# Rows of blocks 2 to 5: added through diagonals and fp32 products, or two of sixteen by VectorE, in place of accumulated transposes

## The chip, the core and the metric

The kernel runs on one core of a Trainium2 chip. The metric is the device time of one execution in microseconds; lower is better. The profile is one execution recorded by the hardware profiler.

## The reference

The reference is a trunk of two layers over 512 tokens of 1024 channels, all in fp32. Layer 0 mixes the tokens by gated spatial products and sparse attention, layer 1 by a gated linear recurrence (HGRN2) of eight heads. After each mixer comes PEER: every token scores 2 x 128 keys in 8 heads, keeps the 16 best experts of 16384 per head, and adds their outputs:

```
experts = top 16 of (s_top[0][i] + s_top[1][j])      # per token and head
gate    = softmax(best)
act     = gelu(sum_d x[t, d] * u_tab[experts, d])    # one number per token and expert
x      += sum over 128 experts of gate * act * v_tab[experts]
```

So each token gathers 128 rows of u and 128 rows of v (1024 floats each) in each layer. A last RMS norm ends the trunk.

## The kernel before

Tokens lie on the 128 partitions. The work is cut into 1024 slots: slot s is one expert of each of 128 tokens. 128 slots make a block (`BLOCK`; 128 tokens of one layer, blocks 0 to 3 for layer 0, 4 to 7 for layer 1), 16 slots a routing unit, and 256 slots a phase (`PHASE`). In every slot:

- POOL (L677) issues an indirect DMA that gathers, for 128 tokens, the u and v rows side by side (8 KB each, 1 MB in all) into one of 8 buffers of `region_g`. Before it issues slot s, it waits until slot s - 8 has been freed (`row_freed`).
- DVE (L1323) multiplies the u half with the normed tokens and sums: the dot product.
- ACT (L943, L944) takes its gelu and multiplies it with the gate, which gives the weight of the row.
- Then the weighted v half is added to the block's sum, in one of three ways. By diagonal: ACT (L956) writes an identity scaled by the weight into `diag`, and PE (L1845) multiplies it with the v half in two fp32 products of 512 columns that accumulate in two PSUM banks. By VectorE (`on_dve`): DVE (L1332) adds weight times v to `x_res`, two slots later, and frees the buffer. By transposes (blocks in `TURNED`, 2 to 5): ACT (L951) scales the 1024 values of the v half in place, and PE (L1851) takes it through eight accumulating 128 x 128 transposes.

Before the change, slots 0 to 191 have VectorE add rows 5, 7, 9 and 13 of each sixteen (`ATTENDED_ROWS`), all other rows of blocks 0, 1, 6 and 7 go by diagonal, and blocks 2 to 5 go by transposes alone. The sum of such a block lies transposed in PSUM: at the next block's second slot DVE copies it out to `sumT` (L1338), PE turns it back (L1860), and one slot later DVE adds it to the residual (L1348, `block_out`); PE's first row of the new block waits for that.

Everything else (attention, the recurrence's heads, the routing of the next blocks) is cut into small pieces with tick numbers. `Threads.run(s)` lays the pieces that are due before, or behind, slot s's own work on every engine, so each engine has a fixed order of instructions. In phases 1 and 2 (slots 256 to 767, blocks 2 to 5) the eight heads of the recurrence come first, one every 19 slots (`HEAD_PACE`) from tick 20 on, then the routing of the next 256 tokens, one head every 7 slots. A head of the recurrence is a chain over engines: projections on PE in 16 of the 19 slots (L1702, L1705), tanh and exponentials on ACT (L896 to L908), decays on DVE (L1118 to L1162) and POOL (L642), level products on PE (L1752), copied out by DVE (L1135), the output product on PE (L1809, L1810), ACT's squares, a root on POOL (L561), and DVE's last scaling (L1206). Phase 3 (slots 768 to 1023) has rows only.

Of the kernel before, what the change touches and what calls it, by code (L numbers as in the profile page):

```python
# [4 lines left out]
D_MODEL = 1024  # L5
SEQ = 512
DEPTH = 2
P = 128
TB = SEQ // P
KC = D_MODEL // P  # L10
# [13 lines left out]
TOPK = 16  # L24
NKEYS = 128
ROW = 2 * D_MODEL
NBUF = 8
HALF = 2 * P
BLOCK = P_HEADS * TOPK
# [6 lines left out]
ATT = 102  # L36
HEADS_AT, HEAD_PACE = 20, 19
EVEN_AT = (-1000, 0)
DVE_ROWS = ((), (), (), ())
ATTENDED = range(192)  # L40
ATTENDED_ROWS = (5, 7, 9, 13)
TURNED = range(2, 6)
FINAL_SLOTS = (3 * PHASE + 20, 3 * PHASE + 24, 3 * PHASE + BLOCK + 8)


# [34 lines left out]
def build(nc, x, wcol_mix, w_ffn, w_fin, w_even, ln_w, ws_t, b_s, pos, ck1, ck2, cv1, cv2, w_out_e,  # L80
# [5 lines left out]
    ACT = mybir.ActivationFunctionType  # L86
    AXX = mybir.AxisListType.X

    with ExitStack() as ctx:
        def sb(name, shape, dt=fp32):  # L90
            return ctx.enter_context(nc.sbuf_tensor(name, shape, dt))

        def sem(name):
            return ctx.enter_context(nc.semaphore(name))

        def event(name):
            return Event(sem(name))

        def carve(region, at, *shape):
            n = 1  # L100
            for s in shape:
                n *= s
            v = region[:, at:at + n]
            if len(shape) == 2:
                v = v.rearrange("p (a b) -> p a b", a=shape[0])
            if len(shape) == 3:
                v = v.rearrange("p (a b c) -> p a b c", a=shape[0], b=shape[1])
            return v
# [18 lines left out]
        X = sb("x_res", [P, TB + 1, D_MODEL])  # L127
        ident_t = sb("ident", [P, P])
        ident = ident_t[:]
# [8 lines left out]
        PS = ctx.enter_context(nc.psum_tensor("ps", [P, 8, 512], fp32))  # L138
# [10 lines left out]
        wts = ta(2 * TOPK)  # L149
# [54 lines left out]

        gath = carve(RG, 0, NBUF, ROW)
        diag = X[:, TB, :].rearrange("p (a b) -> p a b", a=NBUF)
        sumT = X[:, TB, :]
        th = taker(RH)
        XNr = [th(D_MODEL) for _ in range(3)]
        wrow = th(D_MODEL)  # L210
# [56 lines left out]
            event(n) for n in ("o_done", "oss_ready", "og_ready", "ogT_done", "ogT_out", "pw_done", "res_out"))  # L267
        pw_used = event("pw_used")
        routed, gexp_in, gexp_out = event("routed"), event("gexp_in"), event("gexp_out")
        dots_ready, w_ready, scaled_row = event("dots_ready"), event("w_ready"), event("scaled_row")  # L270
        slot_done, vd_done = event("slot_done"), event("vd_done")
        acc_out, f_ss, fin_done = event("acc_out"), event("f_ss"), event("fin_done")
        sumT_out, sum_back = event("sumT_out"), event("sum_back")
        gathered = [sem(f"gathered{i}") for i in range(NBUF)]
        slab_in = [sem(f"slab_in{i}") for i in range(6)]
        ffn_in, fin_in, stored = sem("ffn_in"), sem("fin_in"), sem("stored")
# [3 lines left out]
        def after(eng, ev, n):  # L280

            if n >= 0:
                eng.wait_ge(ev.sem, ev.at(n))
# [10 lines left out]
        def v3(ap, a):  # L294
            return ap.rearrange("p (a b) -> p a b", a=a)
# [26 lines left out]
        def on_dve(s):  # L322
            return s % TOPK in (ATTENDED_ROWS if s in ATTENDED else DVE_ROWS[s // PHASE])

# [5 lines left out]
        def pe_n(s):  # L330

            return pe_rows[s + 1] - 1

        def dve_n(s):

            return dve_rows[s + 1] - 1
# [349 lines left out]
        def _(act):  # L686
            a = nc.scalar
# [249 lines left out]
            def weigh(s):  # L937
                n, k = s // TOPK, s % TOPK
                c = (n % 2) * TOPK + k
                if k == 0:  # L940
                    act.wait_ge(routed.sem, routed.at(n))
                act.wait_ge(dots_ready.sem, dots_ready.at(s))
                link(a.activation(gact[:, c:c + 1], dots[:, c:c + 1], ACT.Gelu_apprx_tanh))  # L943
                i = a.activation(wts[:, c:c + 1], gact[:, c:c + 1], ACT.Copy, scale=gate[:, n % 2, k:k + 1])  # L944
                if on_dve(s):
                    i.then_inc(w_ready.sem, 1)
                else:
                    link(i)
                    if s // BLOCK in TURNED:
                        v_ = gath[:, s % NBUF, D_MODEL:ROW]  # L950
                        a.activation(v_, v_, ACT.Copy, scale=wts[:, c:c + 1]).then_inc(scaled_row.sem, 1)  # L951
                    else:
                        after(act, slot_done, pe_n(s) - NBUF)
                        if s == BLOCK * TURNED.stop:
                            act.wait_ge(sum_back.sem, sum_back.at(len(TURNED) - 1))
                        a.activation(diag[:, pe_n(s) % NBUF, :], ident, ACT.Copy, scale=wts[:, c:c + 1]  # L956
                                     ).then_inc(scaled_row.sem, 1)

            def final_squares(b):
                act.wait_ge(acc_out.sem, acc_out.at(TB + b))  # L960
# [23 lines left out]
        def _(dve):  # L984
            v = nc.vector
# [292 lines left out]
            def gates_of(n):  # L1278

                e = n % 2  # L1280
                m = link.mark(v.scalar_tensor_tensor(experts[:, e * TOPK:(e + 1) * TOPK], esel[:, 0, :], float(NKEYS),
                                                     esel[:, 1, :], ALU.mult, ALU.add))
                dve.wait_ge(gexp_out.sem, gexp_out.at(n))
                link(v.reciprocal(gstat[:, 2:3], gstat[:, 1:2]))
                if n >= 2:
                    after(dve, scaled_row, pe_n(TOPK * (n - 1) - 1))
                link.need(m)
                v.tensor_scalar(gate[:, e, :], gexp, gstat[:, 2:3], None, ALU.mult).then_inc(routed.sem, 1)

# [42 lines left out]
                v.scalar_tensor_tensor(xb, gath[:, s % NBUF, D_MODEL:ROW], wts[:, c:c + 1], xb, ALU.mult, ALU.add  # L1332
                                       ).then_inc(vd_done.sem, 1)

            def sums_out(b):

                after(dve, slot_done, pe_n(BLOCK * (b + 1) - 1))
                v.tensor_copy(v3(sumT, 2), PS[:, 0:2, :]).then_inc(sumT_out.sem, 1)  # L1338

            def block_out(b):  # L1340

                if b in TURNED:
                    dve.wait_ge(sum_back.sem, sum_back.at(TURNED.index(b)))
                else:
                    after(dve, slot_done, pe_n(BLOCK * (b + 1) - 1))
                after(dve, vd_done, dve_n(BLOCK * (b + 1) - 1))
                xb = v3(X[:, b % TB, :], 2)
                v.tensor_tensor(xb, xb, PS[:, 0:2, :], ALU.add).then_inc(acc_out.sem, 1)  # L1348
# [19 lines left out]
            for s in range(SLOTS):  # L1368
                n, k = s // TOPK, s % TOPK
                dot_product(s)  # L1370
                if s >= 2 and on_dve(s - 2):
                    row_added(s - 2)
                if s % BLOCK == 1 and s // BLOCK - 1 in TURNED:
                    sums_out(s // BLOCK - 1)
                if s > BLOCK and s % BLOCK == (2 if s // BLOCK - 1 in TURNED else 1):
                    block_out(s // BLOCK - 1)
                if k < 7:
                    late_ranking(n + 1, k)
                if k >= 12:
                    early_ranking(n + 2, k - 12)  # L1380
                threads.run(s)
                if s - 3 in FINAL_SLOTS:
                    final_norm(FINAL_SLOTS.index(s - 3))
                if k == TOPK - 1:
                    link.need(link.n)
                    link.reset()
# [6 lines left out]
        def _(pe):  # L1393
            t = nc.tensor
# [438 lines left out]
            def row_product(s):  # L1833

                b = s // BLOCK
                first = all(on_dve(r) for r in range(b * BLOCK, s))
                last = all(on_dve(r) for r in range(s + 1, (b + 1) * BLOCK))
                if first and b:
                    if b - 1 in TURNED:
                        sums_turned(b - 1)  # L1840
                    after(pe, acc_out, b - 1)
                pe.wait_ge(scaled_row.sem, scaled_row.at(pe_n(s)))
                if b not in TURNED:
                    for j in range(2):
                        i = t.matmul(PS[:, j, :], diag[:, pe_n(s) % NBUF, :],  # L1845
                                     gath[:, s % NBUF, D_MODEL + j * 512:D_MODEL + (j + 1) * 512], start=first,
                                     stop=last)
                    i.then_inc(slot_done.sem, 1)
                    return
                for c in range(KC):  # L1850
                    i = t.matmul(PS[:, c // 4, c % 4 * P:(c % 4 + 1) * P],  # L1851
                                 gath[:, s % NBUF, D_MODEL + c * P:D_MODEL + (c + 1) * P], ident,
                                 start=first and c % 4 == 0, stop=last, is_transpose=True, skip_group_check=True)
                i.then_inc(slot_done.sem, 1)

            def sums_turned(b):

                pe.wait_ge(sumT_out.sem, sumT_out.at(TURNED.index(b)))
                for c in range(KC):
                    i = t.transpose(PS[:, c // 4, c % 4 * P:(c % 4 + 1) * P], sumT[:, c * P:(c + 1) * P], ident)  # L1860
                i.then_inc(sum_back.sem, 1)

            pe.wait_ge(half_set, 1)
            threads = Threads(mixers(), routings())
# [74 lines left out]
```

## Time and profile before

| | |
|---|---|
| median of 3 runs | 3049.19 us (3046.82 to 3049.41) |
| the profiled execution's own time | 3053.3 us |
| its span, first to last instruction | 3051.6 us |
| PE busy | 2499.6 us (82%) |
| DVE busy | 2162.8 us (71%) |
| ACT busy | 1863.7 us (61%) |
| POOL busy | 1312.8 us (43%) |
| moved by the DMA engines | 1194.80 MB, mean 392 GB/s |
| mean granted TensorE clock | 0.918 |

Busy shares are those of an engine over the span. The 16 DMA engines are shown by the mean share of time that they are busy, which can come out a little over 1. The rows in the section below are by stretches of the span, in microseconds from its start; block 2 begins at about 976 us and block 6 at about 2400 us.

### The profile page before, as it was taken

How to read it: one execution, taken by the hardware profiler on the slowest of the kernel's cores; microseconds unless marked ns; L12 is line 12 of the kernel's file. 1: busy time of each engine (PE TensorE's matmuls, PEld its weight loads, DVE VectorE, ACT ScalarE, POOL GpSimd, SP SyncE). 2: the span in 40 equal slices, each digit the busy share in tenths (PEclk: the TensorE clock that was granted, in tenths of full speed). 3: DMA queues.
4: the chain of work that ended last, by engine and by line, in shares of the span. 5: the costliest groups of instructions: out<-in, count | busy, mean ns of one | idle time of the engine just before them, and what ended most of it. 6: DMA issues, size and time to landing. Idle time of an engine off the chain costs nothing.

```text
span 3051.6 us, 34233 instructions
## 1 busy us (share of the span) xinstructions
PE 2499.6 (82%) x10640; PEld 1632.3 (53%) x10640; DVE 2162.8 (71%) x5501; ACT 1863.7 (61%) x4096; POOL 1312.8 (43%) x1255
## 2 busy tenths in 40 slices
PE   8979799899898777877887778788778778788777
PEld 6445554344464676766576667676567422222222
DVE  0337668898756788878666788888766766677664
ACT  1424244786444888888667788878776544444443
POOL 0014234354444554545433545455434544444342
PEclk8979899999899998889888889889889899999999
DMA  8019999999999999999999999999999999999997
GB/s 288 14 62 425 381 404 425 400 359 377 424 423 427 422 420 418 413 399 416 421 423 426 426 420 422 417 411 417 414 423 424 421 426 427 427 425 424 424 425 318
DMA packets 192661, 1194.80 MB, mean 392 GB/s; under 512 B 21344, under 2 KB 28512, under 8 KB 54752
## 3 DMA queue, kind: packets, MB, share of 16 engines
q0 software_dynamic: 147456, 1073.81, 84.5%
q1 hardware_dynamic: 45024, 118.82, 10.1%
q8 instruction: 84, 1.38, 0.2%
q14 instruction: 97, 0.79, 0.1%
HBM read 1189.38 MB, written 2.10 MB: 390 GB/s over the span
## 4 chain that ended last, share of the span: by engine, by line
DMA 33%; PE 32%; DVE 16%; ACT 13%; issue 4%; POOL 1%; DVEq 0%; POOLq 0%; SPq 0%; ACTq 0%
DMA region_g<-in_uv_dram,experts 30%; PE ps L1845 11%; DVE region_g L1323 8%; PE ps L1673 4%; PE ps L1851 4%; ACT region_g L951 3%; PE ps L1734 2%; ACT region_a L944 1%; DMA region_a<-in_keys_dram 1%; ACT L943 1%; PE ps L1705 1%; DVE region_a L1135 1%; PE ps L1541 1%; DMA region_a<-in_w_even_dram 1%; PE ps L1702 1%
## 5 line engine op out<-in xcount | busy, mean ns | idle before, releaser
L677 POOL DMA_INDIRECT region_g<-in_uv_dram,experts x1024 | 1182.2, 1155 | 1503.8 <-PE ps L1845 668.0
L1323 DVE CUSTOM_DVE_ANT_0 region_g<-region_g,region_h 128x1024 f32<-128x1024 f32 x1024 | 1255.9, 1229 | 560.0 <-DMA region_g<-in_uv_dram,experts 551.0
L1845 PE MATMUL ps<-region_g,x_res 128*128 128x512 f32 x1856 | 913.5, 625 | 178.4 <-ACT x_res L956 171.6
L1851 PE MATMUL ps<-ident,region_g 128*128 128x128 f32 x4096 | 612.2, 301 | 248.5 <-ACT region_g L951 237.1
L943 ACT ACTIVATE region_a<-region_a 128x1 f32<-128x1 f32 x1024 | 204.3, 200 | 872.2 <-DVE region_a L1323 867.5
L1851 PEld LDWEIGHTS ps<-ident,region_g 128*128 128x128 f32 x4096 | 524.9, 155 | 346.6 <-ACT region_g L951 306.4
L1845 PEld LDWEIGHTS ps<-region_g,x_res 128*128 128x128 f32 x1856 | 339.9, 195 | 672.4 <-ACT x_res L956 375.1
L951 ACT ACTIVATE region_g<-region_g,region_a 128x1024 f32<-128x1024 f32 x512 | 588.5, 1149 | 16.7
L944 ACT ACTIVATE region_a<-region_a,gate 128x1 f32<-128x1 f32 x1024 | 301.7, 295 | 33.3
L1673 PE MATMUL ps<-region_a 128*128 128x256 f32 x1024 | 252.1, 392 | 9.0 <-DMA region_a<-in_keys_dram 7.8
L1673 PEld LDWEIGHTS ps<-region_a 128*128 128x128 f32 x1024 | 197.3, 198 | 55.9 <-issue 23.5
L956 ACT ACTIVATE x_res<-ident,region_a 128x128 f32<-128x128 f32 x464 | 186.3, 401 | 20.3 <-PE ps L1860 5.2
L1702 PE MATMUL ps<-region_a 128*128 128x256 f32 x512 | 157.1, 440 | 0.0
L943 ACT ACT_TABLE_LOAD x112 | 143.7, 1283 | 14.0 <-DVE region_a L1323 12.0
L1705 PE MATMUL ps<-region_a 128*128 128x256 f32 x512 | 132.0, 383 | 0.0
L1702 PEld LDWEIGHTS ps<-region_a 128*128 128x128 f32 x512 | 106.1, 229 | 11.3
L1734 PE MATMUL ps<-region_a 128*128 128x512 f32 x192 | 94.5, 619 | 0.0
L1705 PEld LDWEIGHTS ps<-region_a 128*128 128x128 f32 x512 | 89.0, 193 | 7.3
L1323 DVE DVE_READ_ACCUMULATOR2_ANT region_a<- 128x1 f32 x1024 | 83.2, 81 | 0.0
L935 ACT ACT_TABLE_LOAD x63 | 80.8, 1283 | 1.1
L642 POOL TENSOR_TENSOR region_a<-region_a 128x128 f32<-128x128 f32 x112 | 69.1, 634 | 17.0 <-ACT region_a L908 15.9
L1752 PEld LDWEIGHTS ps<-region_a 128*128 128x128 f32 x512 | 67.5, 194 | 2.9
(244 smaller groups left out, 2424.4 us busy)
## 6 DMA issues: line engine op xcount, KB each, us to landing
region_a<-in_w_q_dram SPq DMA_DIRECT2D x32, 1024.0 KB, 21.1
region_a<-in_w_odd_dram SPq DMA_DIRECT2D x32, 1024.0 KB, 9.8
region_g<-in_uv_dram,experts POOLq DMA_INDIRECT x1024, 14.5
region_g<-in_w_even_dram SPq DMA_DIRECT2D x8, 1024.0 KB, 12.0
region_a<-in_w_even_dram SPq DMA_DIRECT2D x8, 1024.0 KB, 16.1
region_a<-in_w_out_o_dram SPq DMA_DIRECT2D x8, 1024.0 KB, 12.0
region_a<-in_keys_dram SPq DMA_DIRECT2D x32, 128.0 KB, 24.2
region_g<-in_w_out_e_dram SPq DMA_DIRECT2D x4, 1024.0 KB, 4.7
```

The lines of the kernel that those rows point to most:

```text
L677: g.indirect_dma_start(out=gath[:, s % NBUF, :], out_offset=None, in_=uv[s // (2 * PHASE)], in_offset=bass.IndirectOffsetOnAxis(ap=experts ...
L943: link(a.activation(gact[:, c:c + 1], dots[:, c:c + 1], ACT.Gelu_apprx_tanh))
L944: i = a.activation(wts[:, c:c + 1], gact[:, c:c + 1], ACT.Copy, scale=gate[:, n % 2, k:k + 1])
L951: a.activation(v_, v_, ACT.Copy, scale=wts[:, c:c + 1]).then_inc(scaled_row.sem, 1)
L956: a.activation(diag[:, pe_n(s) % NBUF, :], ident, ACT.Copy, scale=wts[:, c:c + 1]).then_inc(scaled_row.sem, 1)
L1323: v.tensor_tensor_reduce(out=u_, in0=u_, in1=XNr[n // P_HEADS % 3], scale=1.0, scalar=0.0, op0=ALU.mult, op1=ALU.add, accum_out=dots[:, c: ...
L1673: i = t.matmul(PS[:, 4, p * HALF:(p + 1) * HALF], W[c // 4][:, c % 4, h % 2 * HALF + p * P:h % 2 * HALF + (p + 1) * P], hTh[:, c, :], star ...
L1702: i = t.matmul(PS[:, 2, o * HALF:(o + 1) * HALF], W[:, c % 4, o * P:(o + 1) * P], hTh[:, c, :], start=c == 0, stop=c == KC - 1)
L1705: i = t.matmul(PS[:, 3, o * HALF:(o + 1) * HALF], hTh[:, c, o * P:(o + 1) * P], W[:, c % 4, HALF:2 * HALF], start=c == 0, stop=c == KC - 1)
L1734: i = t.matmul(PS[:, out_bank(o, bank), :], headT[:, c, r * P:(r + 1) * P], W[:, c % 2, half_ * 512:(half_ + 1) * 512], start=c == 0, stop ...
L1845: i = t.matmul(PS[:, j, :], diag[:, pe_n(s) % NBUF, :], gath[:, s % NBUF, D_MODEL + j * 512:D_MODEL + (j + 1) * 512], start=first, stop=last)
L1851: i = t.matmul(PS[:, c // 4, c % 4 * P:(c % 4 + 1) * P], gath[:, s % NBUF, D_MODEL + c * P:D_MODEL + (c + 1) * P], ident, start=first and ...
```

## The change

All rows of blocks 2 to 5 go by diagonal and two fp32 products, but for rows 5 and 13 of each sixteen, which VectorE adds. The scaling of the row by ACT, the transposes, the copy of the transposed sum, its turning back and the waits that belong to them are gone; the block's sum is added one slot earlier. The tanh forms of the sigmoids stay as they were. The heart of the diff:

```diff
-DVE_ROWS = ((), (), (), ())
+DVE_ROWS = ((), (5, 13), (5, 13), ())
-TURNED = range(2, 6)
@@ weigh(s), ACT
-                    if s // BLOCK in TURNED:
-                        v_ = gath[:, s % NBUF, D_MODEL:ROW]
-                        a.activation(v_, v_, ACT.Copy, scale=wts[:, c:c + 1]).then_inc(scaled_row.sem, 1)
-                    else:
-                        after(act, slot_done, pe_n(s) - NBUF)
-                        if s == BLOCK * TURNED.stop:
-                            act.wait_ge(sum_back.sem, sum_back.at(len(TURNED) - 1))
-                        a.activation(diag[:, pe_n(s) % NBUF, :], ident, ACT.Copy, scale=wts[:, c:c + 1]
-                                     ).then_inc(scaled_row.sem, 1)
+                    after(act, slot_done, pe_n(s) - NBUF)
+                    a.activation(diag[:, pe_n(s) % NBUF, :], ident, ACT.Copy, scale=wts[:, c:c + 1]
+                                 ).then_inc(diag_ready.sem, 1)
@@ DVE
-            def sums_out(b):
+            def block_out(b):
 
                 after(dve, slot_done, pe_n(BLOCK * (b + 1) - 1))
-                v.tensor_copy(v3(sumT, 2), PS[:, 0:2, :]).then_inc(sumT_out.sem, 1)
...
-                if s % BLOCK == 1 and s // BLOCK - 1 in TURNED:
-                    sums_out(s // BLOCK - 1)
-                if s > BLOCK and s % BLOCK == (2 if s // BLOCK - 1 in TURNED else 1):
+                if s % BLOCK == 1 and s > BLOCK:
                     block_out(s // BLOCK - 1)
@@ row_product(s), PE
-                for c in range(KC):
-                    i = t.matmul(PS[:, c // 4, c % 4 * P:(c % 4 + 1) * P],
-                                 gath[:, s % NBUF, D_MODEL + c * P:D_MODEL + (c + 1) * P], ident,
-                                 start=first and c % 4 == 0, stop=last, is_transpose=True, skip_group_check=True)
+                for j in range(2):
+                    i = t.matmul(PS[:, j, :], diag[:, pe_n(s) % NBUF, :],
+                                 gath[:, s % NBUF, D_MODEL + j * 512:D_MODEL + (j + 1) * 512], start=first, stop=last)
                 i.then_inc(slot_done.sem, 1)
```

The event `scaled_row` is renamed `diag_ready`, also where DVE waits for it before it overwrites the gates.

## Rows read from the trace of the kernel before

**Rows 1.** Stretches: length, busy PE, PEld, DVE, ACT, POOL, then clock, DMA share, GB/s

```profile
500.00:600.00 100.00, 82.67 (x219) 36.17 (x218) 86.01 (x196) 63.42 (x159) 42.54 (x37) 0.93 1.00 411
600.00:800.00 200.00, 182.59 (x531) 83.39 (x530) 175.65 (x391) 139.35 (x334) 100.41 (x98) 0.95 0.95 379
800.00:900.00 100.00, 99.33 (x341) 61.39 (x340) 64.83 (x167) 45.52 (x129) 39.80 (x36) 1.00 1.02 424
1000.00:1400.00 400.00, 315.05 (x1980) 277.44 (x1979) 331.95 (x913) 333.82 (x606) 208.12 (x205) 0.90 1.00 415
1500.00:1700.00 200.00, 154.34 (x888) 133.13 (x888) 126.74 (x324) 138.56 (x252) 80.00 (x72) 0.85 1.02 424
2500.00:3000.00 500.00, 401.41 (x803) 142.91 (x801) 345.48 (x872) 216.35 (x651) 211.58 (x203) 0.97 1.01 424
```

**Rows 2.** Gathers (L677) from issue to landing in 600:800, 1000:1400 and 2500:3000

```profile
L677 POOL DMA_INDIRECT region_g<-in_uv_dram,experts x71: 932/959/2132, 599.0 to 799.8; - x71
DMA to landing us min/median/max: 5.2/9.3/17.7
...
L677 POOL DMA_INDIRECT region_g<-in_uv_dram,experts x143: 934/984/2164, 1000.8 to 1398.7; - x143
DMA to landing us min/median/max: 5.8/12.8/19.6
...
DMA to landing us min/median/max: 10.8/15.0/17.6
```

**Rows 3.** Waits of DVE in 1000:1400: total us, times, longest us

```profile
DVE region_a L1125 <- ACT region_a L908: 19.5, 7, 3.9
DVE region_g L1323 <- DMA region_g<-in_uv_dram,experts: 14.6, 21, 1.5
DVE region_a L1206 <- POOL ost L561: 10.2, 5, 3.4
DVE region_a L1135 <- PE ps L1752: 4.4, 3, 3.0
DVE region_a L1206 <- issue: 2.3, 1, 2.3
```

**Rows 4.** Groups by line in 1000:1400: busy us, mean ns, idle before

```profile
L1851 PE MATMUL ps<-ident,region_g 128*128 128x128 f32 x1146 | 168.9, 297 | 74.3 <-ACT region_g L951 71.4 <-DVE x_res L1348 2.7
L951 ACT ACTIVATE region_g<-region_g,region_a 128x1024 f32<-128x1024 f32 x143 | 164.4, 1150 | 4.7
```

**Rows 5.** Diagonals, whole span (page), and VectorE's adds with who waits for them

```profile
L956 ACT ACTIVATE x_res<-ident,region_a 128x128 f32<-128x128 f32 x464 | 186.3, 401 | 20.3 <-PE ps L1860 5.2
...
L1332 DVE SCALAR_TENSOR_TENSOR x_res<-region_g,region_a,x_res x48: 1275/1280/1341, 248.4 to 795.5; 128x1024 f32<-128x1024 f32 x48
...
  POOL region_g L677: 78.8, 25
```

**Rows 6.** Chain of waits in 1100:1250, PE working back to back: start, us, records

```profile
1173.50 0.87 PE ps L1705 x4
1174.37 0.89 PE ps L1752 x8
1175.26 0.87 PE ps L1851 x8
```

**Rows 7.** Chain of waits in 800:900, PE working back to back

```profile
812.72 1.72 PE ps L1845 x4
814.44 1.73 PE ps L1673 x8
816.16 3.43 PE ps L1845 x8
```

**Rows 8.** Timeline at the boundary of blocks 2 and 3 (DVE, then PE)

```profile
1334.36 1.23 DVE L1338 COPY x_res<-ps 128x1024 f32<-128x1024 f32 x1 [0.21 <-PE ps L1851]
1338.36 1.21 DVE L1348 TENSOR_TENSOR x_res<-x_res,ps 128x1024 f32<-128x1024 f32 x1
...
1335.91 1.04 PE L1860 MATMUL ps<-ident,x_res 128*128 128x128 f32 x8
1339.63 1.42 PE L1851 MATMUL ps<-ident,region_g 128*128 128x128 f32 x8 [2.68 <-DVE x_res L1348]
```

**Rows 9.** Stretches around three boundaries, columns as in rows 1

```profile
1340.00:1360.00 20.00, 16.60 (x103) 14.61 (x102) 14.66 (x38) 17.10 (x35) 10.81 (x10) 0.85 0.86 325
2040.00:2080.00 40.00, 32.39 (x198) 28.61 (x197) 34.20 (x86) 32.35 (x63) 22.49 (x20) 0.84 0.98 382
1680.00:1700.00 20.00, 12.75 (x56) 10.27 (x56) 15.77 (x41) 13.65 (x27) 9.50 (x6) 0.59 1.01 426
```

More of the change, by code:

```diff
@@ L206, in build @@
         diag = X[:, TB, :].rearrange("p (a b) -> p a b", a=NBUF)
-        sumT = X[:, TB, :]
         th = taker(RH)
@@ L269, in build @@
         routed, gexp_in, gexp_out = event("routed"), event("gexp_in"), event("gexp_out")
-        dots_ready, w_ready, scaled_row = event("dots_ready"), event("w_ready"), event("scaled_row")
+        dots_ready, w_ready, diag_ready = event("dots_ready"), event("w_ready"), event("diag_ready")
         slot_done, vd_done = event("slot_done"), event("vd_done")
         acc_out, f_ss, fin_done = event("acc_out"), event("f_ss"), event("fin_done")
-        sumT_out, sum_back = event("sumT_out"), event("sum_back")
         gathered = [sem(f"gathered{i}") for i in range(NBUF)]
@@ L1285, in gates_of @@
                 if n >= 2:
-                    after(dve, scaled_row, pe_n(TOPK * (n - 1) - 1))
+                    after(dve, diag_ready, pe_n(TOPK * (n - 1) - 1))
                 link.need(m)
@@ L1333, in row_added @@
                                        ).then_inc(vd_done.sem, 1)
-            def sums_out(b):
+            def block_out(b):
                 after(dve, slot_done, pe_n(BLOCK * (b + 1) - 1))
-                v.tensor_copy(v3(sumT, 2), PS[:, 0:2, :]).then_inc(sumT_out.sem, 1)
[L1340 to L1345, printed above, removed]
                 after(dve, vd_done, dve_n(BLOCK * (b + 1) - 1))
@@ L1837, in row_product @@
                 last = all(on_dve(r) for r in range(s + 1, (b + 1) * BLOCK))
[L1838 to L1849, printed above, removed]
-                for c in range(KC):
-                    i = t.matmul(PS[:, c // 4, c % 4 * P:(c % 4 + 1) * P],
-                                 gath[:, s % NBUF, D_MODEL + c * P:D_MODEL + (c + 1) * P], ident,
-                                 start=first and c % 4 == 0, stop=last, is_transpose=True, skip_group_check=True)
-                i.then_inc(slot_done.sem, 1)
[L1856 to L1861, printed above, removed]
+                if first:
+                    if b:
+                        after(pe, acc_out, b - 1)
+                pe.wait_ge(diag_ready.sem, diag_ready.at(pe_n(s)))
+                for j in range(2):
+                    i = t.matmul(PS[:, j, :], diag[:, pe_n(s) % NBUF, :],
+                                 gath[:, s % NBUF, D_MODEL + j * 512:D_MODEL + (j + 1) * 512], start=first, stop=last)
+                i.then_inc(slot_done.sem, 1)
             pe.wait_ge(half_set, 1)
```

## The prediction

> **What bounds the kernel now.** I read the stretches first [rows 1]. From slot 256 to 767 (blocks 2 to 5, about 976 to 2400 us) the 16 DMA engines are busy all the time: share 1.00 to 1.02, 415 to 424 GB/s, as in the last phase (1.01, 424), where a core does little but gather and add rows. The transfers set the pace, and an engine matters only when rows are given back so late that the gather queue runs dry. How near that is differs by stage. In the stretch with the heads of the second layer (1000 to 1400) PE is 79% busy at a granted clock of 0.90, DVE 83%, ACT 83%. Stretch 600 to 800, where VectorE adds four rows of sixteen beside the attention, shows an over-filled stage: PE 91%, DVE 88%, DMA share 0.95. Stretch 800 to 900 shows PE at 99% with clock 1.00, DVE 65%, and DMA still at 1.02: a full PE alone starves nothing.
>
> The time from a gather's issue to its landing says how deep the queue is: median 15.0 us in the last phase, 12.8 among the heads, 9.3 in the starved stretch, and 5.2 to 5.8 for one that lands with nothing ahead of it [rows 2]. A slot takes 400/143 = 2.80 us among the heads, so eight buffers are 22.4 us of rows. Of these 5.8 are an empty queue's latency, so rows must be free some 16 us after landing at the latest, less in practice; today 22.4 - 12.8 = 9.6 us are used.
>
> Then who waits on DVE among the heads [rows 3]. Only 14.6 us of 400 are waits for a row to land; that is DVE's true slack, 14.6/143 x 19 = 1.9 us per head of 19 slots (53.1 us). The other waits are inside a head: 19.5 for ACT's exponentials (2.6 per head), 10.2 + 2.3 for the root that hangs on PE's output product (1.7 per head), 4.4 for PE's levels. So DVE, 83% busy, is filled much more than it looks.
>
> **The change, part by part** (at the profiled execution's own time, 3053.3 us, span 3051.6; the median of the runs is 3049.2, so 4.1 lower).
>
> ACT: 512 scalings of a row at 1.15 us go [rows 4], 448 diagonals at 0.40 us come [rows 5]: 589 - 180 = 409 us less work. ACT is not the end of anything by itself; what it gives is 0.75 us earlier per row, and per head one such step before the exponentials: I take 0.75 us off DVE's wait there.
>
> DVE: 2 x 32 = 64 adds at 1.28 us [rows 5], 82 us in all; 19/8 x 1.28 = 3.0 us per head. An add stands in DVE's queue after the dot product two slots later, and ahead of that slot's ranking step, head piece and the next dot product; ACT's gelu and so PE wait behind it. In the 208 of 512 slots that hold no head (the routing stage, 1500 to 1700, and its twin) DVE is 63% busy [rows 1] and the adds hide under the waits for rows. Gone are four copies at 1.23 us and four slots' shift of the block sum.
>
> PE: a row by eight transposes takes 0.87 us at full clock [rows 6], a row by two fp32 products 1.72 us [rows 7]. Per head, transposed rows are 19 x 0.87 = 16.5 us; 7/8 of them by products are 16.6 x 1.72 = 28.6. The head's own work: 64 projection records (four are 0.87) 13.9 us, 32 level records (eight are 0.89) 3.6 us, some 16 small records of the same width, estimated 1.8; 19.3. So PE goes from 35.8 to 47.9 us of 53.1, from 67% to 90% at full clock. Routing stage: a head in 7 slots is 32 records (6.9 us) and 8 small (0.9), 7.8 + 10.5 = 18.3 us in 7 x 2.8 = 19.6: 93%, beside a DVE at 63%; that is the picture of 800 to 900, which ran at full DMA rate. I cost that stage at nothing; if the cover failed it would be one slot's lateness, below 3 us.
>
> Block boundaries: today the first row of the next block waits until VectorE has copied the sum, PE turned it back, DVE done another dot product and the add [rows 8]: copy at 1334.4, PE goes on at 1339.6. The DMA share falls to 0.86 in the 20 us around it (0.15 x 20 = 3.0 us lost) and to 0.98 in 40 us around the twin (1.2 us); at the other boundary it stays 1.01 [rows 9]. The change ends this: PE waits for one add. Gain 4.2 us; none if the fuller engines eat it.
>
> The price among the heads, 16 of them: added work 3.0, less the slack 1.9, less ACT's 0.75: +0.4 us per head. On top comes PE's lateness. PE's row step is 0.85 us longer, and for 16 of a head's 19 slots it has 0.87 + 0.33 + 1.50 = 2.70 us of work per 2.80 us slot. Today PE waits 71 of 400 us for scaled rows [rows 4], after ACT's exponentials above all, and catches up after it at 1 us per slot; afterwards it catches up at 0.1. So it reaches the head's output product late, and behind that hang ACT's squares, POOL's root and DVE's L1206, which DVE already waits for. No row shows this wait with a fuller PE. Bounds per head: 0 (the lateness stays within the two slots between PE's pieces and their users) and 4 us (what the exponentials hold up, not recovered). I take 1.1, near the added row step of 0.85, as the wait at L1206 is now 1.7 and not a multiple of it. Together 1.45 x 16 = 23 us.
>
> Sum: 3053.3 + 23 - 4 = 3072; less 4.1, **3068 us**.
>
> Of PE's clock, rows show 0.90 among the heads with PE 79% busy and 1.00 at 99% busy [rows 1]; its two levels are 2.4 and 1.2 GHz. At an unchanged mean of 0.90 the demand would be 47.9/0.90 = 53.2 us of 53.1, no room at all; at 1.00 there are 5.2 us of room per head. The forecast stands between: the clock comes up, but lateness remains.
>
> **Rivals.**
> 1. Starvation, as in 600 to 800. For it: after the change PE (90%) and DVE (83% + 3.0/53.1 = 89%) stand where they stand there (91%, 88%), and rows added by DVE come free two slots late: POOL waited 78.8 us on such adds [rows 5]. Against: there four rows of sixteen are DVE's, here two, and ACT falls from 83% to some 55% (1.15 against 7/8 of 0.40 us in each 2.80). Price: 1.015 - 0.95 = 6.5 us per 100, over some 860 us of heads 56 us: 3053.3 + 56 - 4.2 - 4.1 = 3101.
> 2. PE's lateness never reaches DVE: the clock comes back to 1.00 as in 800 to 900, PE's 5.2 us of room per head catch up what the exponentials hold, and only DVE's 0.4 us per head stays: 3053.3 + 6.4 - 4.2 - 4.1 = 3051; with the adds hidden in buffers as well, 3045. For it: the DMA share of 1.00 to 1.02 almost everywhere. Against: PE's idle time cannot be placed where rows need it, since its order is fixed. The Trainium skill (TensorE: Matmul & The Clock Gate, the part on the clock gate) says that the throttled clock is the resting state and that activity releases it; by that rule this rival's clock follows from the change itself. The step from 0.90 at 79% to 1.00 at 99% agrees.
> 3. Faster: ACT is the engine that makes rows late today (its 1.15 us scaling is queued behind the exponentials, and PE waits 71 us per 400 for it). With it 0.75 us earlier and catching up faster, the queue stays deeper and the share rises from 1.00 to 1.02 among the heads: 0.02 x 860 = 17 us at the most, 6 as a third of it, with the boundaries 10: 3039. It decides if the time from landing to freeing falls by more than the 0.85 us that PE adds.
>
> **How the numbers follow.** The forecast (DVE and PE late together, 3053 to 3085) 0.45; rival 1 0.22; rival 2 0.20; rival 3 0.13. About 0.2% (6 us) is what a measurement of this kernel can tell from no change. Slower: 0.43 of the forecast's 0.45 (its lowest end is no change) and rival 1's 0.22: 0.65. Same: most of rival 2 and that low end: 0.20. Faster: rival 3 and a little of rival 2: 0.15. The range reaches down to rival 3's 3039 and up just past rival 1, 3103; the likeliest case alone is 3053 to 3085.
>
> **What would show it.** Right: L1323's wait for landed rows among the heads near 0, DVE at 88 to 90% there, PE at 90% or more with the clock at 0.95 or above, issue to landing down from 12.8 to 10 to 12 us, DMA share 0.97 to 0.98 among the heads and 1.01 elsewhere, and no hole at the block boundaries; ACT's total near 1455 us. The head stretch (slots 288 to 448) takes longer, the routing stretch as long as now. Wrong if the share stays 1.00 to 1.01 among the heads (rival 2), if issue to landing grows (rival 3), or if PE's clock stays at 0.90 and PE is 99% busy, which would make the loss PE's alone. The diagonals and adds themselves should show 0.40 and 1.28 us; if the adds take more, the term of 3.0 us per head grows with them.

## The result, and the profile after

The changed kernel takes 3098.26 us (median of 4 runs, 3092.31 to 3102.72) against 3049.3 us before (now 4 runs): ratio 1.0156, 95% interval 1.0144 to 1.0169. It is 49 us slower; the forecast was 19 us slower. The profiled execution has a span of 3093.8 us, 42 us more than before. In the code of after, the gather is L674, the dot product L1314, VectorE's add L1323, the diagonal L947, the row product L1824, and the last scaling of a head on DVE is L1197 (L1206 before).

The stretches, with the columns of [rows 1]:

```profile
600.00:800.00 200.00, 181.96 (x536) 83.41 (x534) 176.76 (x393) 140.35 (x337) 100.30 (x97) 0.96 0.95 379
1000.00:1400.00 400.00, 361.45 (x1261) 218.88 (x1261) 337.74 (x893) 216.97 (x566) 198.15 (x200) 0.97 0.99 400
1500.00:1700.00 200.00, 183.11 (x596) 106.92 (x595) 135.36 (x317) 84.26 (x243) 87.81 (x76) 0.98 1.02 424
2500.00:3000.00 500.00, 394.94 (x800) 138.48 (x798) 348.78 (x886) 216.77 (x651) 210.90 (x205) 0.99 1.01 424
```

Only the stretch with the heads lost: 415 GB/s before, 400 now. Counted by slots in the two profiled executions (starts of the dot products), slots 276 to 431, which hold the heads of blocks 2 and 3, take 460.0 us where they took 438.1, and slots 532 to 687, with those of blocks 4 and 5, 462.2 where they took 435.7: 48 us more in these two stretches. The stretches behind them, which hold the routing, are 3 us shorter each. Routing (1500 to 1700) moves 424 GB/s as before, with PE at 92%. DVE is 84% busy among the heads, hardly more than the 83% before.

PE's mean granted clock came up among the heads, from 0.90 at 79% busy to 0.97 at 90%. The direction agrees with the clock gate's rule that activity releases the throttle (the Trainium skill, TensorE: Matmul & The Clock Gate, the part on the clock gate). But the busy share alone doesn't set it: the last phase, whose rows were products before the change too, had 0.97 at 80% busy [rows 1]. Whether the kind of record or the way in which the idle time is spread makes the difference, no run here separates. PE still has a tenth of its time idle among the heads, at nearly full clock.

Gathers among the heads, their count in 1000 to 1400 and the time to landing, against 143 gathers and a median of 12.8 us in [rows 2]; then, from the view of waits, what POOL's gather issues waited for, before (L677) and after (L674):

```profile
L674 POOL DMA_INDIRECT region_g<-in_uv_dram,experts x138: 932/982/2060, 999.4 to 1399.7; - x138
DMA to landing us min/median/max: 5.3/9.9/14.8
```

```profile
POOL region_g L677 <- PE ps L1851: 167.3, 108, 5.8
...
POOL region_g L674 <- PE ps L1824: 152.6, 91, 5.1
POOL region_g L674 <- DVE x_res L1323: 32.7, 14, 6.0
```

Five rows fewer in 400 us, and gathers that land 9.9 us after their issue, nearer the 5.3 of the quickest: rows come free too late. From the end of a row's dot product to the issue that refills its buffer, the mean over the slots with heads rose from 5.5 to 6.8 us. POOL's waits for PE's rows are no longer than before; those for VectorE's are new. What DVE waits for in the same stretch, total us, times, longest, against [rows 3]:

```profile
DVE region_a L1197 <- POOL ost L558: 19.5, 5, 6.0
DVE region_a L1197 <- issue: 6.5, 1, 6.5
DVE region_g L1314 <- DMA region_g<-in_uv_dram,experts: 6.0, 9, 1.2
```

The wait for landed rows, DVE's slack, went from 14.6 to 6.0 us; the wait for the head's root doubled, from 12.5 to 26.0. Over the whole span, the rows of that wait, first before (L1206), then after (L1197), each with the engine that ended it:

```profile
  POOL ost L561: 32.7, 12
  issue: 15.1, 4
```

```profile
  POOL ost L558: 54.4, 12
  issue: 33.3, 4
```

47.8 us before, 87.7 now: 40 us more, while the span grew by 42. One of the two longest of the sixteen waits (9.1 us; the other is 9.6) shows how it comes about. Timeline of the changed kernel, by engine:

```profile
1475.00 0.20 ACT L914 ACTIVATION_READ_ACCUMULATOR region_a<-ps 128x1 f32 x1
...
1476.10 1.88 PE L1715 MATMUL ps<-region_a 128*128 128x512 f32 x4
...
1481.25 1.88 PE L1824 MATMUL ps<-region_g,x_res 128*128 128x512 f32 x4
...
1476.54 0.94 POOL L674 DMA_INDIRECT region_g<-in_uv_dram,experts  x1 [3.17 <-PE ps L1824]
1479.97 0.94 POOL L674 DMA_INDIRECT region_g<-in_uv_dram,experts  x1 [2.50 <-PE ps L1824]
1483.40 0.94 POOL L674 DMA_INDIRECT region_g<-in_uv_dram,experts  x1 [2.50 <-PE ps L1824]
1484.41 0.22 POOL L557 TENSOR_SCALAR ost<-ost 128x2 f32<-128x2 f32 x1
1484.71 0.72 POOL L558 TENSOR_TENSOR ost<-ost,half 128x2 f32<-128x2 f32 x1
...
1485.53 0.61 DVE L1197 SCALAR_TENSOR_TENSOR region_a<-ps,ost,region_a 128x128 f32<-128x128 f32 x2 [9.09 <-issue]
```

ACT has the sums of squares ready at 1475.2. POOL takes their root only at 1484.4: its own order has the root (tick 19 of the head) behind three gather issues, the last of which waits until PE has freed the row of the head's slot 19, 1483.1. DVE, whose scaling stands after the dot product of slot 21, sits idle for 9.1 us, and no dot product is done meanwhile. So a row that PE frees late stops the engine that all later rows need.

The other heads look the same. In all sixteen of the changed kernel, POOL begins the root 1.0 us after it began the gather issue that waits for slot 19's row, and that is 4.2 to 9.2 us after ACT's squares ended (median 5.8). The order was there before the change: in 14 of the 16 heads of the kernel before, the root also began 1.0 us after that issue, but only 1.1 to 6.4 us after the squares (median 2.9). The same head in the kernel before (the profile marks its wait "issue", though the scaling begins 0.1 us after POOL's root has ended, at 1463.1):

```profile
1455.82 0.20 ACT L917 ACTIVATION_READ_ACCUMULATOR region_a<-ps 128x1 f32 x1
1461.07 0.94 POOL L677 DMA_INDIRECT region_g<-in_uv_dram,experts  x1 [1.66 <-PE ps L1851]
1462.08 0.22 POOL L560 TENSOR_SCALAR ost<-ost 128x2 f32<-128x2 f32 x1
1463.21 0.61 DVE L1206 SCALAR_TENSOR_TENSOR region_a<-ps,ost,region_a 128x128 f32<-128x128 f32 x2 [4.87 <-issue]
```

Last, the answers to [rows 5] and to the block boundaries of [rows 9] (the sums of blocks 2 and 4 are now added at 1352.2 and 2090.1 us):

```profile
L947 ACT ACTIVATE x_res<-ident,region_a 128x128 f32<-128x128 f32 x912 | 366.2, 402 | 29.8
L1323 DVE SCALAR_TENSOR_TENSOR x_res<-region_g,region_a,x_res 128x1024 f32<-128x1024 f32 x112 | 144.5, 1290 | 2.9 <-ACT region_a L941 2.9
```

```profile
1340.00:1360.00 20.00, 20.00 (x90) 13.93 (x89) 19.27 (x51) 6.28 (x22) 11.64 (x13) 1.00 1.00 409
2060.00:2100.00 40.00, 39.22 (x139) 24.67 (x140) 36.28 (x96) 18.90 (x50) 22.50 (x21) 0.93 1.00 408
```

The operations cost what was expected of them, and the holes at the boundaries are filled.

### The profile page after: what moved, and what is told of

Its sections match the earlier page's. It is cut to its first block, busy times and chain, and to the rows that moved or that the text cites. A ratio compares the mean times of both kernels' runs of the same rounds, so it can differ in the third digit from the quotient of the medians.

```text
span 3093.8 us, 30069 instructions
## 1 busy us (share of the span) xinstructions
PE 2704.8 (87%) x8304; PEld 1442.2 (47%) x8304; DVE 2235.9 (72%) x5561; ACT 1472.6 (48%) x4032; POOL 1312.3 (42%) x1255
## 4 chain that ended last, share of the span: by engine, by line
PE 46%; DMA 26%; DVE 15%; ACT 6%; issue 4%; POOL 2%; DVEq 0%; POOLq 0%; SPq 0%; ACTq 0%
PE ps L1824 24%; DMA region_g<-in_uv_dram,experts 23%; DVE region_g L1314 7%; PE ps L1654 5%; PE ps L1686 3%; PE ps L1715 2%; POOL region_g L674 2%; PE ps L1683 1%; PE ps L1733 1%; DMA region_a<-in_keys_dram 1%; DVE x_res L1323 1%; DMA region_a<-in_w_even_dram 1%; ACT x_res L947 1%; PE ps L1522 1%; PE ps L1613 1%
## 5 line engine op out<-in xcount | busy, mean ns | idle before, releaser
L1824 PE MATMUL ps<-region_g,x_res 128*128 128x512 f32 x3648 | 1779.9, 619 | 269.3 <-ACT x_res L947 254.6
L674 POOL DMA_INDIRECT region_g<-in_uv_dram,experts x1024 | 1174.6, 1147 | 1561.4 <-PE ps L1824 1255.2
L1314 DVE CUSTOM_DVE_ANT_0 region_g<-region_g,region_h 128x1024 f32<-128x1024 f32 x1024 | 1260.5, 1233 | 499.8 <-DMA region_g<-in_uv_dram,experts 489.4
L1824 PEld LDWEIGHTS ps<-region_g,x_res 128*128 128x128 f32 x3648 | 671.0, 195 | 1091.2 <-issue 541.0
L947 ACT ACTIVATE x_res<-ident,region_a 128x128 f32<-128x128 f32 x912 | 366.2, 402 | 29.8
L1654 PE MATMUL ps<-region_a 128*128 128x256 f32 x1024 | 246.3, 386 | 7.5 <-DMA region_a<-in_keys_dram 6.3
L1654 PEld LDWEIGHTS ps<-region_a 128*128 128x128 f32 x1024 | 197.8, 194 | 80.6 <-issue 51.3
L1323 DVE SCALAR_TENSOR_TENSOR x_res<-region_g,region_a,x_res 128x1024 f32<-128x1024 f32 x112 | 144.5, 1290 | 2.9 <-ACT region_a L941 2.9
L1683 PE MATMUL ps<-region_a 128*128 128x256 f32 x512 | 134.9, 394 | 1.0 <-DVE region_a L1150 1.0
L1686 PE MATMUL ps<-region_a 128*128 128x256 f32 x512 | 129.1, 379 | 0.0
L1314 DVE DVE_READ_ACCUMULATOR2_ANT region_a<- 128x1 f32 x1024 | 83.9, 82 | 0.0
L639 POOL TENSOR_TENSOR region_a<-region_a 128x128 f32<-128x128 f32 x112 | 78.4, 719 | 4.1 <-ACT region_a L905 2.6
L1197 DVE SCALAR_TENSOR_TENSOR region_a<-ps,ost,region_a 128x128 f32<-128x128 f32 x32 | 9.8, 347 | 87.7 <-POOL ost L558 54.4
L1126 DVE COPY_PREDICATED region_a<-level_mask,ps 128x256 f32<-128x256 int32 x128 | 56.6, 442 | 16.2 <-PE ps L1733 7.5
## 6 DMA issues: line engine op xcount, KB each, us to landing
region_g<-in_uv_dram,experts POOLq DMA_INDIRECT x1024, 13.2
region_g<-in_w_even_dram SPq DMA_DIRECT2D x8, 1024.0 KB, 11.7
```

The source lines that it names most:

```text
L674: g.indirect_dma_start(out=gath[:, s % NBUF, :], out_offset=None, in_=uv[s // (2 * PHASE)], in_offset=bass.IndirectOffsetOnAxis(ap=experts ...
L1314: v.tensor_tensor_reduce(out=u_, in0=u_, in1=XNr[n // P_HEADS % 3], scale=1.0, scalar=0.0, op0=ALU.mult, op1=ALU.add, accum_out=dots[:, c: ...
L1654: i = t.matmul(PS[:, 4, p * HALF:(p + 1) * HALF], W[c // 4][:, c % 4, h % 2 * HALF + p * P:h % 2 * HALF + (p + 1) * P], hTh[:, c, :], star ...
L1683: i = t.matmul(PS[:, 2, o * HALF:(o + 1) * HALF], W[:, c % 4, o * P:(o + 1) * P], hTh[:, c, :], start=c == 0, stop=c == KC - 1)
L1686: i = t.matmul(PS[:, 3, o * HALF:(o + 1) * HALF], hTh[:, c, o * P:(o + 1) * P], W[:, c % 4, HALF:2 * HALF], start=c == 0, stop=c == KC - 1)
L1824: i = t.matmul(PS[:, j, :], diag[:, pe_n(s) % NBUF, :], gath[:, s % NBUF, D_MODEL + j * 512:D_MODEL + (j + 1) * 512], start=first, stop=last)
```

## The experiments

Theory A: the gate just shown, POOL's root behind the gather issue that waits for slot 19's row. Theory B: load. DVE's 82 us of adds and PE's longer rows fill the engines, and the wait for the root is only where that shows. Ratios are to the kernel before, run on the same chip; its medians there were 3051.0, 3051.9 and 3051.4 us in the three sets.

**The two parts alone.** The adds with transposed rows; then the products with no row added by VectorE:

```diff
 # kernel before
-DVE_ROWS = ((), (), (), ())
+DVE_ROWS = ((), (5, 13), (5, 13), ())
```

> The kernel before (rows of blocks 2 to 5 by transposes, sums turned back), with rows 5 and 13 of each sixteen added by VectorE. Theory A (the gate: DVE's last scaling of each head waits for POOL's root, and that root stands behind the gather issue that waits until the row two slots earlier is free; the change made the row free later): the 64 adds alone leave PE's rows short, so the wait for the root grows only where the freed row is one of DVE's; about 3049 + 5 to 15 = 3054 to 3064. Theory B (DVE's load: 82 us of adds against little slack): most of the 49 us comes with the adds alone, 3080 to 3095.

```diff
 # changed kernel
-DVE_ROWS = ((), (5, 13), (5, 13), ())
+DVE_ROWS = ((), (), (), ())
```

> The changed kernel with no row of blocks 2 to 5 added by VectorE: all 16 of 16 by diagonal and products. PE's demand per head rises to 19 x 1.72 + 19.3 = 52.0 us of 53.1. Theory A: PE frees rows still later, the root's wait stays as in the changed kernel or grows, 3095 to 3125. Theory B (DVE's load): DVE is relieved of 82 us, and the time falls to 3055 to 3070, unless PE itself is the bound.

The adds alone: 3070.09 us, ratio 1.0063 (1.0044 to 1.0082), 19 us: between the two ranges, 6 us above A's and 10 below B's. The wait for the root hardly grew (51.3 us over the span, 47.8 before), so these 19 us did not come through it. The products alone: 3110.33 us, ratio 1.0191 (1.0170 to 1.0212), 59 us, more than the whole change. The wait for the root in the kernel with products alone (L1197, over the span):

```profile
  POOL ost L558: 84.7, 12
  issue: 38.8, 4
```

123.5 us. So the products alone make a loss, a larger one than the change, and beside them the adds take 10 us off it. Each add spares PE a row, which may be why; no run tests that by itself.

**The gate moved.** POOL's root of each head two ticks earlier; all the work is done:

```diff
-                    yield head_tick(q, h) + 19
+                    yield head_tick(q, h) + 17
                     pool.wait_ge(oss_ready.sem, oss_ready.at(n))
```

> The changed kernel with POOL's root of each head put at tick 17 of the head, was 19, so that it stands behind the gather issue that waits for the row of slot 17 and not of slot 19. No work is left out. Theory A: the root ends up to two slots (5.6 us) earlier, DVE's wait for it (87.7 us over 16 heads) falls below 40, and the time falls by 15 to 40 us, to 3058 to 3083. Theory B (DVE and PE are simply full, the wait is only where it shows): DVE then waits elsewhere, 3093 to 3100.

3056.03 us, ratio 1.0016 (1.0006 to 1.0026): of 49 us, some 43 are gone, a little past theory A's range (3058 to 3083). DVE's wait for the root over the span, and the stretch with the heads (141 gathers there now):

```profile
  POOL ost L558: 13.6, 9
  issue: 12.2, 4
```

```profile
1000.00:1400.00 400.00, 371.65 (x1322) 228.58 (x1321) 351.00 (x928) 222.30 (x582) 210.48 (x202) 0.97 1.00 411
```

The wait fell from 87.7 to 25.8 us. PE and DVE are now busier per microsecond (93% and 88%), with as much work as in the changed kernel: they were not full. The same move in the kernel before:

> The kernel before with the same move of POOL's root from tick 19 to 17. Theory A: DVE's wait for it (47.8 us over 16 heads) falls to 10 to 20, but rows are free early enough here, so only the few us that the DMA engines lose among the heads can come back: 3040 to 3049. Theory B: no change, 3049, or a little slower as POOL waits for ACT's squares with a gather behind it, up to 3055.

3050.96 us, ratio 1.0002 (0.9991 to 1.0014): no change, above theory A's range, although the wait fell from 47.8 to 11.7 us. The last two lines are two other waits of DVE, for ACT's tanh and for landed rows:

```profile
  POOL ost L561: 9.5, 7
  issue: 2.2, 2
...
DVE region_a L1155 <- ACT region_a L896: 26.7, 16, 3.2
DVE region_g L1323 <- DMA region_g<-in_uv_dram,experts: 552.6, 554, 6.5
```

Of the 36 us that the wait for the root gave up, 25 came back as waits for ACT: for its tanh (L1155, 9.4 us in the kernel before; L1162, 8.6 there and 13.2 here) and its exponentials (L1125, 41.7 and 44.9). The wait for landed rows stayed at 551.0 and 552.6. With transposed rows and ACT's long step, the root was not the only thing that held DVE. The same move with the products alone:

> All rows of blocks 2 to 5 by diagonal and products, none by VectorE, root at tick 17. Theory A: the root's wait (123 us over 16 heads with tick 19) falls by 60 or more and the time from 3110 to 3060 to 3080; what stays above 3056 is PE itself (52.0 us of products and pieces per head of 53.1) and DVE's waits for the level products. Theory B: PE is the bound, 3100 to 3110.

3060.31 us, ratio 1.0028 (1.0016 to 1.0041), 50 of 59 us gone. PE with 52 of 53 us of work per head costs at most some 8 us over the kernel before, net of what the change gives back elsewhere. Not all of the gate is gone here: DVE still waits 43.9 us for the root, nearly the 47.8 of the kernel before, and 16.0 us for the level products (8.0 there).

**How the loss follows the tick.** The changed kernel with ticks 18 and 16:

> The changed kernel with POOL's root at tick 18 (19 gave 3098, 17 gave 3056). Theory A: one slot of the two; between them, 3068 to 3082. Theory B (the pace among the heads is set elsewhere, and tick 17 helped by another order on POOL): at either end, 3056 or 3098.

> The changed kernel with POOL's root at tick 16. Theory A: the root then waits on ACT's squares themselves, which come at tick 19, and with it the gather issues behind it on POOL; nothing more to gain, 3052 to 3062. If an earlier root still gains, the gate was not yet gone: 3045 to 3050.

Tick 18: 3075.85 us, ratio 1.0094 (1.0065 to 1.0122). Tick 16: 3059.76 us, ratio 1.0036 (1.0016 to 1.0056). So 19, 18, 17, 16 give 3098, 3076, 3056, 3060: a slot is worth some 20 us down to tick 17. Between 17 and 16 the times can't be told apart; there the root comes to stand on ACT's squares themselves, and POOL waits with the gathers behind it (POOL's waits among the heads, tick 16):

```profile
POOL ost L557 <- ACT region_a L914: 9.3, 6, 3.0
```

**The gate made later, nothing else.** The kernel before, tick 20:

> The kernel before with POOL's root put one tick later, at 20, so behind the gather issue that waits for the row of slot 20; no arithmetic and no other order is changed. Theory A: DVE waits up to 2.8 us more per head, 47.8 + 45 = 93 us as in the changed kernel, and the time rises by 20 to 45 us, to 3070 to 3095, without one added instruction. Theory B: 3049 to 3056.

3063.02 us, ratio 1.0040 (1.0024 to 1.0056), 11 us slower without an added instruction: the direction of A, but below its range. The wait and the wait for landed rows over the span:

```profile
  POOL ost L561: 58.9, 12
  issue: 25.2, 4
```

```profile
DVE region_g L1323 <- DMA region_g<-in_uv_dram,experts: 530.1, 520, 6.7
```

The wait grew by 36 us to 84.1, nearly the changed kernel's 87.7, yet 21 of them came out of the wait for rows (551.0 before, page). So the wait alone isn't the loss: here 36 us more of it cost 11 us, with the products alone 76 us more cost 59. The adds are not what makes it dearer, for the kernel with products alone has none; one thing that differs is PE, which has next to no room there to catch up. That this is the reason is likely, but no run shows it by itself.

**The adds.** With transposed rows, does the same move take off their 19 us?

> Transposed rows with rows 5 and 13 of each sixteen added by VectorE, and POOL's root at tick 17 of each head, was 19. Theory A (the gate): the 19 us that the adds cost alone also come through the root's wait (33 of 47.8 us per run were already there and each add makes it later), so they go: 3048 to 3055. Theory B (load): the 19 us are DVE's added work and stay: 3065 to 3072.

3069.52 us, ratio 1.0069 (1.0045 to 1.0093): no, theory A fails here and B holds, though the wait for the root did fall, to 15.2 us. In its place DVE waits for ACT's tanh (L1155) and exponentials:

```profile
DVE region_a L1125 <- ACT region_a L908: 36.7, 16, 3.7
DVE region_a L1155 <- ACT region_a L896: 21.0, 14, 3.2
DVE region_a L1206 <- issue: 8.1, 4, 2.6
DVE region_a L1206 <- POOL ost L561: 7.1, 6, 2.0
```

The adds did not lengthen these waits, which were 26.7 and 44.9 us with the same move and no adds. They took the room beside them: DVE waits 512.0 us for landed rows here and 552.6 there. But the full change with this move had the same adds and lost only 5 us. Among what differs is ACT's step, 1.15 us against 0.40. So ACT's scaling was cut, in the kernel with adds, transposes and tick 17:

```diff
-                        v_ = gath[:, s % NBUF, D_MODEL:ROW]
+                        v_ = gath[:, s % NBUF, D_MODEL:D_MODEL + P]
```

> Transposed rows with two of sixteen added by VectorE and the root at tick 17, where ACT scales 128 columns of a row and not 1024, so that its step takes some 0.4 us as a diagonal does. It leaves out the scaling of the other 896 columns, so its output isn't the reference's. With the full scaling this cost 18 us over the kernel before; with diagonals and products 5 us. If ACT's long step is what makes the adds cost 18 us (DVE waits for tanh and exponentials of the head, which stand behind the scalings): 3043 to 3056. If the adds cost it by DVE's own load: 3065 to 3072.

3055.93 us, ratio 1.0021 (1.0007 to 1.0034): 14 of 18 us gone. The step, in 1000 to 1400, and the waits over the span:

```profile
L951 ACT ACTIVATE region_g<-region_g,region_a 128x128 f32<-128x128 f32 x125 | 50.2, 402 | 4.1
```

```profile
DVE region_a L1125 <- ACT region_a L908: 24.0, 15, 3.0
DVE region_a L1155 <- ACT region_a L896: 4.3, 4, 1.7
```

DVE's wait for landed rows is back at 545.2 us. So ACT's long step was needed for the loss: DVE's adds and its waits for ACT together were more than its room, while the waits without the adds cost nothing and the adds with short waits cost 5 us. Two things stay open. A short step also lets PE free a row some 0.75 us earlier, and this run doesn't separate that from the shorter wait for ACT. And there is no run with the short step and no adds, so what the adds cost beside it isn't measured. With diagonals and products at tick 17 the kernel with adds and the one without (3056 and 3060 us) can't be told apart.

**The boundaries alone.** The kernel before, without `sums_out` and `sums_turned`:

```diff
-                if s % BLOCK == 1 and s // BLOCK - 1 in TURNED:
-                    sums_out(s // BLOCK - 1)
-                if s > BLOCK and s % BLOCK == (2 if s // BLOCK - 1 in TURNED else 1):
+                if s > BLOCK and s % BLOCK == 1:
                     block_out(s // BLOCK - 1)
...
-                    if b - 1 in TURNED:
-                        sums_turned(b - 1)
```

> The kernel before without the copy of the transposed sum and without turning it back: the transposed sum is added as it stands at the next block's second slot. It leaves out the turning back of the sums of blocks 2 to 5, so its output isn't the reference's. It prices the block boundaries alone: 4 us by the prediction (3.0 + 1.2 of DMA idle time), 3043 to 3047; if the buffers take the boundary up, 3049.

3046.05 us, ratio 0.9985 (0.9973 to 0.9997), some 4.5 us (1 to 8 by the interval), and the hole is filled:

```profile
1340.00:1360.00 20.00, 14.89 (x94) 12.25 (x95) 15.36 (x44) 19.38 (x38) 9.46 (x10) 0.91 1.00 411
```

No kernel that does all the work beat the one before by more than the noise.

## Why the prediction was wrong

The direction was right, the size was not: 19 us forecast, 49 measured. By its steps:

- DMA engines set the pace outside the heads; routing, with PE at 92%, costs nothing: right. It moves 424 GB/s before and after.
- The boundaries give 4.2 us back: right; 4.5 alone, within a wide interval.
- Costs of the operations (0.40 and 1.28 us, PE 90% busy among the heads): right; ACT's total is 1472.6 us where 1455 was forecast. But DVE was forecast 88 to 90% busy among the heads and was 84%: it stood idle and was not loaded. The +0.4 us per head that the adds were to cost with ACT's relief taken off can't be seen once the root is moved: products alone lose 8 us with tick 17, and with adds it is 5.
- The step that failed: PE's lateness, 1.1 us per head, within bounds of 0 and 4. DVE's wait for the root alone grew by 40/16 = 2.5 us per head, and the move of the root to tick 17 gave 43/16 = 2.7 back. The bound of 4 held, and the place was right (L1206, behind ACT's squares and POOL's root), but not the path. The prediction had PE reach the head's output product late, and the root follow it. That did not happen: the squares, which need the output product, ended on average 2.9 us behind the end of slot 19's dot product in the kernel before, and 2.6 us behind it in the changed one.

  What came later is the gather issue that waits for slot 19's row, 5.0 us behind that dot product before and 7.6 us now, and POOL reaches the root only behind it. So the root takes up the whole delay from a dot product to a freed row: ACT, PE's queue, the longer product. In the two heads where VectorE adds slot 19's row, the issue came later still (9.0 and 9.6 us), but the root's lag behind the squares, 6.2 us in both, is near the median of 5.8. The prediction asked of the wait on POOL who produces the data, and not what stands ahead of it in POOL's order. The kernel before had the sign, in the timeline above: the squares end at 1456.0, but POOL is in its gather issues until 1462.0 and takes the root only then.
- Rival 1 (starvation, 3101) came nearest by its number, and its picture is there in part: gathers 9.9 us to landing, POOL waiting 32.7 us on VectorE's adds. But it said that engines of 90% and 89% starve the queue as in 600 to 800, and with tick 17 engines at 93% and 88% move 411 GB/s. That its number came within 3 us is luck.
- Rival 2 (3051) describes what is left when the gate is moved: the clock is at 0.97, where it said 1.00, and PE's room is used, 3056. Rival 3 is refuted: the time to landing shrank.

What stays open is how the last 5 to 8 us of the products at tick 17 divide between the rest of the root's wait, PE's waits and DVE's waits for level products, and why a microsecond of wait for the root costs more with products than with transposes.

## What to carry to other kernels

Before a step is made longer, look for every small instruction that stands, in its own engine's order, behind an instruction waiting for that step's end; above all a few elements of arithmetic on the queue that issues DMAs and waits for free buffers. Such a gate turns latency into lost throughput: here 0.85 us more per row cost 59 us by itself and 49 with the adds, and moving one line by two slots took some 43 of the 49 back. Taking a wait away gains nothing while another stands behind it (the same move was worth nothing before the change), so price added work and all the waits of an engine together against the time that it has left.

## What the runs showed of the hardware

An fp32 transpose of a 128 x 128 block is one record of 0.11 us (eight in 0.87, [rows 6]), and an fp32 product of 512 columns two of 0.43 (four in 1.72, [rows 7]), back to back in stretches with a granted clock of 1.00: the same 1024 columns take twice as long as a product. PE's mean granted clock among the heads was 0.87 to 0.90 with transposed rows at 75 to 80% busy, and 0.97 to 1.00 with products at 90 to 97% busy. So the added products cost PE less than their count: by the prediction's own sum they are 12.1 us per head of 53.1, an estimated 91 us in 400, and PE's busy time grew by 46, with 5 rows fewer.
